# First layer of a two-layer trunk: block products for four of its down groups, and all modulation rows in one turn of its loop

## The reference, cut to what matters

```python
for l in range(2):
    mod = silu(c) @ w_ada[l] + b_ada[l]                 # 6 x 1024 numbers
    sh1, sc1, g1, sh2, sc2, g2 = split(mod, 6)
    h = rms_norm(x, norm1_g[l]) * (1 + sc1) + sh1
    x = x + g1 * (mixer(h) @ w_out[l])                  # convolution and retention
    h2 = rms_norm(x, norm2_g[l]) * (1 + sc2) + sh2
    x = x + g2 * (square(relu(h2 @ w_up[l])) @ w_down[l])   # 1024 -> 4096 -> 1024
return rms_norm(x, final_g)
```

## Time and profile before

| | |
|---|---|
| median of 3 runs | 1144.61 us (1144.42 to 1144.75) |
| profiled execution, its own time | 1145.57 us |
| its span | 1143.8 us |
| TensorE matmul busy | 1128.3 us, 99% |
| VectorE busy | 906.8 us, 79% |
| ScalarE busy | 619.6 us, 54% |
| GpSimd busy | 251.5 us, 22% |
| DMA engines | 162.9 MB, 142 GB/s over the span |

### The profile page before, as it was taken

How to read it: one execution, slowest core, us unless ns; L and a number is a source line. 1 busy time by engine, 2 the same in 40 slices (tenths; PEclk the granted TensorE clock), 3 DMA queues, 4 the chain that set the end, 5 groups by cost and what they waited for, 6 DMA issues and landing times. The chain is left out here.

```text
span 1143.8 us, 19969 instructions
## 1 busy us (share of the span) xinstructions
PE 1128.3 (99%) x6864; PEld 1014.6 (89%) x6864; DVE 906.8 (79%) x1308; ACT 619.6 (54%) x1064; POOL 251.5 (22%) x179
## 2 busy tenths in 40 slices
PE   6999999999999999999999999999999999999998
PEld 4888888998989989989988888889988999999998
DVE  7968888679788587585677788876888899899884
ACT  5655445247455454554553555524646566666665
POOL 4493010310332332422224800104001000000003
PEclk8999999999999999999999999999999999999999
DMA  9874334624444354333408433463242233223322
GB/s 363 323 293 148 110 110 147 221 75 147 130 155 124 127 165 128 127 114 125 130 36 326 171 120 120 135 222 120 93 129 98 88 111 110 92 95 106 110 74 74
DMA packets 45749, 162.87 MB, mean 142 GB/s; under 512 B 5504, under 2 KB 6656, under 8 KB 45184
## 3 DMA queue, kind: packets, MB, share of 16 engines
q1 hardware_dynamic: 45408, 162.10, 41.3%
q10 hardware_dynamic: 288, 0.08, 0.0%
HBM read 160.06 MB, written 2.10 MB: 142 GB/s over the span
## 5 line engine op out<-in xcount | busy, mean ns | idle before, releaser
L1334 DVE TENSOR_TENSOR w_lo<-w_raw,w_hi 128x1024 fp32r<-128x1024 f32 (+1 forms) x190 | 223.1, 1176 | 104.4 <-ACT w_hi L852 102.9
L852 ACT CAST w_hi<-w_raw 128x1024 fp32r<-128x1024 f32 (+1 forms) x186 | 182.6, 983 | 68.3 <-PE ps L421 59.2
L419 PE MATMUL ps<-h_hi,w_hi 128*128 128x512 f32 (+1 forms) x528 | 193.6, 367 | 0.0
L420 PE MATMUL ps<-h_lo,w_hi 128*128 128x512 f32 (+1 forms) x528 | 192.1, 364 | 0.0
L421 PE MATMUL ps<-h_hi,w_lo 128*128 128x512 f32 (+1 forms) x528 | 192.0, 364 | 0.0
L419 PE MATMUL ps<-u_hi,w_hi 128*128 128x512 f32 (+1 forms) x480 | 173.7, 362 | 0.0
L420 PE MATMUL ps<-u_lo,w_hi 128*128 128x512 f32 (+1 forms) x480 | 173.4, 361 | 0.0
L421 PE MATMUL ps<-u_hi,w_lo 128*128 128x512 f32 (+1 forms) x480 | 173.1, 361 | 0.0
L421 PEld LDWEIGHTS ps<-h_hi,w_lo 128*128 128x128 f32 x528 | 99.6, 189 | 16.0
L420 PEld LDWEIGHTS ps<-h_lo,w_hi 128*128 128x128 f32 x528 | 99.7, 189 | 15.1
L419 PEld LDWEIGHTS ps<-h_hi,w_hi 128*128 128x128 f32 x528 | 99.7, 189 | 15.1
(11 more groups left out here) (279 smaller groups left out, 2798.5 us busy)
## 6 DMA issues: line engine op xcount, KB each, us to landing
w_raw<-weights SPq DMA_DIRECT2D x200, 512.0 KB, 3.4
ada_raw<-ada SPq DMA_DIRECT2D x80, 512.0 KB, 4.7
arena<-ada SPq DMA_DIRECT2D x16, 512.0 KB, 15.3
x<-xT SPq DMA_DIRECT2D x2, 1024.0 KB, 7.1
tab<-tables SPq DMA_DIRECT2D x2, 1024.0 KB, 12.8
outT<-x SPq DMA_DIRECT2D x2, 512.0 KB, 3.0
out_rows<-tok_rows SPq DMA_DIRECT2D x4, 256.0 KB, 2.5
tab<-tables SPq DMA_DIRECT2D x1, 512.0 KB, 14.7
```

The lines of the kernel that those rows point to most:

```text
L419: nc.tensor.matmul(out, wh, hi, start=first, stop=False, skip_group_check=True)
L420: nc.tensor.matmul(out, wh, lo, start=False, stop=False, skip_group_check=True)
L852: nc.scalar.copy(w_hi[:, j, cols], w_raw[:, j, cols]).then_inc(w_hi_done, 1)
L1334: nc.vector.tensor_tensor(w_lo[:, j, cols], w_raw[:, j, cols], w_hi[:, j, cols].bitcast(F32), ALU.subtract).then_inc(w_lo_done, 1)
```

## The change

- In the first layer the loop's first turn stays as it was (now unrolled); its other two turns use `both_step` and `down_pair`, as the second layer does. So four of the first layer's down groups become `down_pair`. The weights of these groups are laid out in blocks on the host, as in the second layer.
- The eight pairs of modulation rows 16 to 23 leave the three turns: each `pair_step` q = 0 to 3 of the first turn now reduces two pairs, the old one in its place and another at the end of the step; pair 23 is reduced in the first `both_step`.
- `s_one` (sum S1) lies in `ssum` in the first layer, since silu(c) in `c_act` is still needed; `ssum` is cleared after its last use as S1.
- The sums of weight blocks in the last two turns move from GpSimd to VectorE, but for four at the seam.
- cos and sin are loaded again for the second layer (512 KB), since `u_first` now overwrites them.
- At the end of the first layer the four residuals of the last down group are inside `both_step`; the split of slot 2 follows them. ScalarE's `v_split` waits for the end of the last down group.

The core of the diff:

```diff
+FIRST_TURN = (1, 0)
+TURNS_BEFORE = (-1, 2)
+        s_ones = ssum[:], c_act[:, T:2 * T]
...
+        def counted(l, i, size, count):
+            return i * size + (TURNS_BEFORE[l] * size + count)
...
@@ SyncE
-                if l < 1:
-                    at = slice(HEADS * T, HEADS * T + 2 * T)
-                    sp.dma_start(tab[:, at], tables[:, at]).then_inc(rope_in, 16)
+                if l > 0:
+                    sp.wait_ge(xs_lo, XS_U + 32)
+                at = slice(HEADS * T, HEADS * T + 2 * T)
+                sp.dma_start(tab[:, at], tables[:, at]).then_inc(rope_in, 16)
...
+                if l < DEPTH - 1:
+                    def rows(pair):
+                        for a in range(2):
+                            load_ada(b0 + (2 * pair + a), a, 2)
+                    for q in range(4):
+                        load_step(l, 11 + q, 0, 0, summed=l * 4 * PAIRS + 4 * q + 4,
+                                  rows=(lambda: rows(15 + 2 * q)) if q else None)
+                        rows(16 + 2 * q)
+                with sp.Fori(FIRST_TURN[l], 3) as i:
...
@@ TensorE
+                for i in range(FIRST_TURN[l]):
+                    for q in range(4):
+                        both(i, q, False)
+                with pe.Fori(FIRST_TURN[l], 3) as i:
+                    for q in range(4):
+                        both(i, q, True)
...
@@ ScalarE
-                    pe_has(l, U_LAST - 3)
+                    pe_has(l, U_LAST - 1)
                     act.wait_ge(ada_done, ADAS + SLOTS)
                     v_split(0)
                     v_split(1)
...
@@ VectorE, pair_step
-                    if q == 0:
-                        gate_pair(15, M_GATE2 + 6)
-                    if q in (1, 2):
-                        next_rows()
-                    if q == 3:
-                        with dve.If(i < 2):
-                            next_rows()
+                    gate_pair(*((15 + 2 * q, 2 * (2 * q - 1)) if q else (15, M_GATE2 + 6)))
...
                     split_lo(l, step + 1, 2)
+                    gate_pair(16 + 2 * q, 4 * q)
...
@@ VectorE, after the steps
                 if l < DEPTH - 1:
-                    pair_step(0, 0)
-                    with dve.Fori(0, 3) as i:
-                        for q in range(1, 5):
-                            pair_step(i, q)
...
+                    for q in range(4):
+                        pair_step(0, q)
+                both_step(FIRST_TURN[l], 0)
+                with dve.Fori(FIRST_TURN[l], 3) as i:
+                    for q in range(1, 5):
+                        both_step(i, q)
 
                 if l < DEPTH - 1:
                     dve.wait_ge(mod_added, l * 24 + 32)
                     norm_gain(l * 2 + 2, 0, mod[:, 1:2 * KT:2],
                               par[:, bass.ds(below(l * PARAMS + PARAMS + C_G1, DEPTH * PARAMS, KT), KT)])
-                    residuals(U_LAST - 4, 1)
                 split_lo(l, 23, 3)
...
@@ GpSimd
                 if l < DEPTH - 1:
-                    with pool.Fori(0, 3) as i:
-                        for q in range(4):
-                            next_sums(i, q)
+                    for q in range(4):
+                        next_sums(0, q)
+                    pool.wait_ge(rinv_ps, l * 4 + 3)
                 else:
                     pool.wait_ge(mod_added, l * 24 + 24)
-                    sums_after_pair(0, 0)
+                sums_after_pair(FIRST_TURN[l], 0)
+                if l < DEPTH - 1:
+                    pool.wait_ge(ds_split, counted(l, 2, 16, 24))
+                    clear_sum(l * 2 + 2)
```

More of the change, by code:

```diff
@@ L310, in load_ada, with load_step @@
                              ).then_inc(ada_in[slot], 16)
-            def load_step(l, step, adas, b, since=SLOTS, summed=None, down=None, raw=None):
+            def load_step(l, step, adas, b, since=SLOTS, summed=None, down=None, raw=None, rows=None):
                 also = [None] * SLOTS
@@ L316, in load_step @@
                     also[0] = s_raw, summed
-                    if l == DEPTH - 1:
+                    if l == DEPTH - 1 or not isinstance(step, int) or step > 14:
                         also[1] = s_split, summed
@@ L321, in load_step @@
                 for j in range(SLOTS):
+                    if rows and j == 3:
+                        rows()
                     load_weight(l, step, j, also=also[j])
@@ L609, in pair, with down_pair @@
                         lambda k: h_lo[:, 4 + k, HALVES[1]]).then_inc(pe_unit, 2)
-            def down_pair(u, u_split, evac, group, i, c):
+            def down_pair(u, u_split, evac, group, l, i, c):
                 def product(bank, w_high, w_low, high, low, first=False):
@@ L802, in _, with both @@
                 down(u0 + (U_PLAIN + 4), xs + (XS_U + CHUNK), ed + (2 + ED_DOWN + 4), 0)
-                with pe.Fori(0, 3) as i:
-                    for q in range(4):
[L806 to L813, removed]
+                def both(i, q, blocks):
+                    u = u0 + i * 16 + (U_PAIR + 4 * q)
+                    pair(u, l, i * 4 + (q + 1), ea + i * 12 + (EA_PAIR + 3 * q + 3), blocks)
+                    u_split = xs + i * 8 + (XS_U + 8 + 4 * (q // 2))
+                    evac = ed + i * 16 + (2 + ED_DOWN + 8 + 4 * q)
+                    if blocks and q % 2:
+                        down_pair(u, u_split, evac, 1 - q // 2, l, i, q // 2 + 1)
+                    else:
+                        down(u, u_split, evac, 1 - q // 2)
+                for i in range(FIRST_TURN[l]):
+                    for q in range(4):
+                        both(i, q, False)
+                with pe.Fori(FIRST_TURN[l], 3) as i:
+                    for q in range(4):
+                        both(i, q, True)
                 n, added = l * 2 + 2, l * SQ + SQ_MIX
@@ L1870, in sum_low @@
                     def sum_low(p, at):
-                        split, source = {S1: (3, s_one), S4: (4, w_raw[:, 1, 0:T])}[at]
+                        split, source = {S1: (3, s_ones[l]), S4: (4, w_raw[:, 1, 0:T])}[at]
                         dve.wait_ge(s_raw, l * (4 * PAIRS) + p * 4 + 4)
@@ L1967, in in_turn @@
                         s1_free()
-                        nc.vector.tensor_tensor(s_one, a21, a22, ALU.add).then_inc(done, 1)
+                        nc.vector.tensor_tensor(s_ones[l], a21, a22, ALU.add).then_inc(done, 1)
                         s3_free()
@@ L2204, in in_turn @@
                     s1_free()
-                    nc.gpsimd.tensor_tensor(s_one, a21, a22, ALU.add).then_inc(done, 1)
+                    nc.gpsimd.tensor_tensor(s_ones[l], a21, a22, ALU.add).then_inc(done, 1)
                     s3_free()
```

147 lines of the change are left out of this document (66 added, 81 removed).

## The result

| | median | lowest to highest | runs |
|---|---|---|---|
| before | 1144.62 us | 1144.31 to 1145.44 | 22 |
| after | 1146.24 us | 1145.43 to 1147.82 | 22 |

The ratio is 1.0015 (95% interval 1.0008 to 1.0021): 1.62 us slower, within 0.2% of no change, but 2.5 us above the predicted 1143.75 and outside the range, and to the other side of no change: a gain of 0.9 us was forecast. The runs of after are also spread over 2.4 us, those of before over 1.1.

The account below looks back on a forecast made before the run. The prediction took TensorE, busy 99% of the span, as the bound: -3.3 us for block products and +2.5 for the wait at the mean gave -0.9, so 1143.75 us, range 1141.4 to 1145.4.

Parts of the forecast that it names:

- the seam: First both_step (q=0) of the first layer: no wait of TensorE added, bounds 0 and 0.5 us.
- Block products: Four first-layer down groups become down_pair, 10.08 us each in place of 10.91: 3.3 us less.
- VectorE in the last two turns: First layer's last two turns: VectorE takes over weight sums and adds hidden sums, at no cost.
- two pairs a step: First turn of the first layer: a second modulation pair reduced at each step's end, adding nothing.
- the tables: Reload of cos and sin (512 KB) behind the v weights: hidden, no cost; 3.4 us if uncovered.
- The last part, the chain: After E, the first layer's last down group's end: late residuals and sums of squares, TensorE waits 2.5 us more for the mean.
- The two meetings: Last part: VectorE's last two v_all_lo meet queued GpSimd additions, 0.53 us each; chain ends E + 16.5, at most 17.0.
- case (a): Wait at the mean eats most of the gain: -1.7 to +0.2 us, 1142.9 to 1144.8, chance 0.64.
- Nothing behind gives it back: Behind the first layer's mean: TensorE has no later wait there, so the added 2.5 us stays.
- Case (b): Full gain, chain not late because VectorE clears its queue before E: 1141.3 to 1142.2 us, chance 0.17.
- (d): down_pair slower than 10.08 us because of the fuller VectorE: -1 to +2, 1143.6 to 1146.6 us, chance 0.10.
- Case (c): Last part: slot 1's v weights load late, delaying the mean; over 0.2% slower, up to 1148.6 us, chance 0.06.

Follow-up runs that it names:

- e2_rows_alone: Kernel before with only the modulation rows moved (two pairs a step in the first turn, pair 23 in the step behind): 1145.37 us, ratio 1.0004.
- e2_no_meeting: Kernel after with VectorE's last two v_split moved behind rstd, the first two still ahead of the residuals: 1145.03 us, ratio 1.0002.
- e1_mean_later: Kernel after with the first layer's mean taken two tiles later and the spread of rstd too: 1145.12 us, ratio 1.0006.
- e1_before_delayed: Kernel before with two more 128x1024 VectorE subtractions ahead of the last part's residuals: 1148.85 us, ratio 1.0037.

## Why the prediction was wrong, step by step

- **Block products, -3.3: right.** 10.08 us in each of the four (the other two start at 501.79 and 542.93); -3.28 from the first pair to E.
- **VectorE in the last two turns, two pairs a step, the seam, the tables: nothing, right.** TensorE has no gap up to E. At the seam the margin was thinner than I gave it (`e2_rows_alone`). Behind the v products nothing changed (562.1 us left in both), so the reload of cos and sin is hidden.
- **The last part, the chain: right in its places, a little short in its size.** Tile 0 at E + 7.28 (predicted 7.2), first addition at E + 8.28 (8.2), TensorE ready at E + 13.84 (13.83). Without meetings the last addition ends at E + 15.6 (15.6; in `e2_no_meeting` at 568.43 with E = 552.85). The two meetings lengthened an addition by 0.75 us each, where I took 0.53: 15.6 + 1.5 less 0.2 of pause is 16.9, a wait of 3.1 us, +2.9 where I took +2.5 and had 3.0 as the upper end. That upper end, E + 17.0, is a wrong sum: 15.6 + 2 x 1.1 less 0.2 is 17.6, a wait of 3.8 us and +3.6. With it case (a) would have ended at 1145.4, still below the measured 1146.24. One reading was off too: the GpSimd sum of 2.31 us in the earlier trace rows did not wait for the reduction at 336.40 but for the split that began at 335.25, just ahead of it, and the reduction then waited for the sum; that they take turns stands. The Trainium skill ("SBUF — State Buffer", Who interferes with whom) calls the shared port pair of VectorE and GpSimd an exclusive lock, has a VectorE instruction with two SBUF inputs contend for it, and says, of VectorE's 2-port modes, that whoever issues first keeps it for the whole instruction. The trace agrees as far as that an addition issued 0.5 us into a `v_all_lo` is held up by 0.75, about what was left of its 1.2, and that the residuals, which read PSUM, hold nobody up (additions beside them keep 0.74).
- **The step that failed: "Nothing behind gives it back", with "the second mean and the v products follow at fixed distances".** The first half is true. The second is not: the sum had the wait at its own length only, and took TensorE's pace behind it as given. In the record of after the 3.11 us of idleness were followed by 3.4 us at the lower clock, 1.5 us of loss; filling the idleness gave back 2.0 us in the median. The rows of before could have given the term: behind its 3.41 us of waiting at the start of the program the clock is at 0.50. With the term that is missing: 1143.75 + 0.4 for the larger wait + 2.0 = 1146.2, and 1146.24 was measured (the 2.0 is taken from these runs, so this shows that the parts add up, not that they were foreseen).
- **Case (a)** held in its mechanism, and its upper end of +0.2 was too low by the clock. Case (b) did not come. The time lies within the numbers of (d), 1143.6 to 1146.6, but by chance: its mechanism, block products slower than 10.08, did not come. That the result is within 0.2% of no change, the outcome given 0.72, is no success of the sum either, since a term of 2.0 us was missing from it. Case (c) was near in one respect: ScalarE waited 0.21 us for the load of the second v unit, which it cast at 556.41, 3.4 us behind E, in time.

What is shown: that the drop follows an idle stretch and goes when that stretch is filled, twice, in two kernels (2.0 us in after; the upper group in the other), and that the same idle stretch may or may not bring it. What is not shown: what decides between the executions, and what the slower runs of `e1_mean_later` and the slowest of after have more. The Trainium skill ("TensorE: Matmul & The Clock Gate", Part 1: The HAM clock gate) has the clock step between just two levels by how busy the engine has been; the trace agrees, 1.00 and 0.50, with values between only where a stretch holds both.

## What to carry to other kernels

- A wait on an engine that is otherwise always busy has two prices: its length, and what the clock does behind it. Here idle stretches of 0.2 to 0.7 us cost their length or up to 0.3 more, with no drop of the clock. One of 1.60 us had none behind it in either of two records. Those of 1.8 to 3.1 us were followed by the lower clock in four of five records, which cost 1.5 to 3.1 us more. In a sum for a kernel that is bound by TensorE, add a term for the clock to each new wait of that size, with an upper bound for it.
- A spread that grows (1.1 to 2.4 us here) while the record shows little is a sign of it: ask for the starts of matmuls and the granted clock in stretches of a few us behind each wait, since the row of slices hides them.
- When work is moved ahead of a chain that had no time to spare, look for work in the chain's queue that nobody needs yet. Here the four v splits were such: moved behind the residuals they turned +1.6 us into -2.1.

## What the runs showed of the hardware that was not expected

- In three records the pace fell only 1.2 to 2.2 us after TensorE had resumed: at 571.13 behind the mean of 569.96, at 573.85 behind that of 571.67, at 570.47 behind that of 568.49. It stayed down for 3.2 to 3.4 us there. In that of `e1_before_delayed` (wait 3.05) the granted clock fell at about 573.0, 0.1 us behind the mean of 572.87, and stayed down for 6.8 us. At the start of the kernel before it fell within the wait itself.
- In one program the same wait (1.92 and 1.93 us) was followed by the drop in one execution and by none in another.
- At the lower level matmuls of 256 columns stand 0.21 us apart, against 0.12: about 1.8 times, not 2, while the granted clock is half.
